# A hybrid encoder step whose 64-token sample is taken ahead of the prompt's chunks

## The reference

```
h = RMSNorm_pre(x)
proj = h @ w_in            # 7704 columns: q, k, v of two attentions, gate paths, pooling, 3 x 1024 merge gates
A: GLA linear attention, 4 heads, chunks of 64 in the reference, state (64 x 128) per head
B: causal pooling mixer
C: gated DeltaNet, 4 heads, state (128 x 128) per head:
   u = triangular_solve(1 + M, beta v - ...);  o = q_dec S + a_qk u;  S = g_last S + k_dec^T u
m = sum_b sigmoid(g_b) * (branch_b @ wo_b);   x = x + RMSNorm_post(m @ w_out)
```

## Time and profile before

| | us |
|---|---|
| median of 3 runs | 2552.24 |
| time of the profiled execution | 2555.57 |
| its span, first to last instruction | 2553.8 |
| PE matmul busy | 2476.2 (97%) |
| PE weight load busy | 2384.8 (93%) |
| DVE / ACT / POOL busy | 1041.3 / 674.8 / 820.7 |
| mean granted PE clock | 0.981 |
| bytes moved | 265.88 MB, mean 104 GB/s |

### The profile page before, as it was taken

How to read it: one execution, slowest core, us unless ns; L and a number is a source line. 1 busy time by engine, 2 the same in 40 slices (tenths; PEclk the granted TensorE clock), 3 DMA queues, 4 the chain that set the end, 5 groups by cost and what they waited for, 6 DMA issues and landing times. The chain is left out here.

```text
span 2553.8 us, 40027 instructions
## 1 busy us (share of the span) xinstructions
PE 2476.2 (97%) x15943; PEld 2384.8 (93%) x15943; DVE 1041.3 (41%) x1603; ACT 674.8 (26%) x1349; POOL 820.7 (32%) x711
## 2 busy tenths in 40 slices
PE   7999999999999999999999999999999979999998
PEld 7989999999999999998999999999999869999886
DVE  6620111134465662005554554545555443325332
ACT  6211111111255521113222332222332232223221
POOL 1211221121211212215545555445555213334222
PEclk9999999999999999999999999999999879999999
DMA  4213521111112122411432326432224345553543
GB/s 163 73 68 110 212 76 50 42 52 42 42 51 76 51 82 88 139 59 46 117 110 79 84 82 208 133 100 81 82 81 110 104 165 212 178 183 129 159 144 99
DMA packets 200200, 265.88 MB, mean 104 GB/s; under 512 B 16177, under 2 KB 175297, under 8 KB 194433
## 3 DMA queue, kind: packets, MB, share of 16 engines
q1 hardware_dynamic: 200064, 263.86, 32.1%
HBM read 164.54 MB, written 99.29 MB: 103 GB/s over the span
## 5 line engine op out<-in xcount | busy, mean ns | idle before, releaser
L178 POOL TENSOR_TENSOR w_hi<-w_raw,zero 128x1024 fp32r<-128x1024 f32 x77 | 148.3, 1926 | 1188.9 <-PE dense L348 824.8
L346 PE MATMUL dense<-h_hi_first,w_hi 128*128 128x352 f32 x1032 | 341.2, 331 | 0.7 <-POOL w_lo L180 0.7
L347 PE MATMUL dense<-h_lo_first,w_hi 128*128 128x352 f32 x1032 | 334.1, 324 | 0.0
L347 PE MATMUL dense<-h_lo_second,w_hi 128*128 128x352 f32 x1032 | 334.0, 324 | 0.0
L348 PE MATMUL dense<-h_hi_first,w_lo 128*128 128x352 f32 x1032 | 334.0, 324 | 0.0
L348 PE MATMUL dense<-h_hi_second,w_lo 128*128 128x352 f32 x1032 | 333.2, 323 | 0.0
L346 PE MATMUL dense<-h_hi_second,w_hi 128*128 128x352 f32 x1032 | 332.3, 322 | 0.0
L1360 PE MATMUL gate_bank<-h_hi_first,w_hi 128*128 128x352 f32 x768 | 275.7, 359 | 12.4 <-issue 5.1
L1360 PE MATMUL gate_bank<-h_hi_first,w_lo 128*128 128x352 f32 x768 | 250.4, 326 | 0.0
L1360 PE MATMUL gate_bank<-h_lo_first,w_hi 128*128 128x352 f32 x768 | 250.3, 326 | 0.0
L2205 PE MATMUL y<-o_hi,wo_hi 128*128 128x352 f32 x576 | 187.7, 326 | 14.2 <-DVE wo_lo L2249 12.8
(11 more groups left out here) (234 smaller groups left out, 4765.1 us busy)
## 6 DMA issues: line engine op xcount, KB each, us to landing
w_raw<-in_w_in SPq DMA_DIRECT2D x77, 512.0 KB, 5.8
rows_then_inputs<-scratch_feat SPq DMA_DIRECT2D x16, 1856.0 KB, 9.2
scratch_feat<-row_y SPq DMA_DIRECT2D x28, 1056.0 KB, 4.9
gate<-scratch_gates SPq DMA_DIRECT2D x12, 2112.0 KB, 8.5
scratch_gates<-gate_row SPq DMA_DIRECT2D x96, 176.0 KB, 2.3
o_raw<-scratch_branch_out SPq DMA_DIRECT2D x6, 2112.0 KB, 13.0
scratch_merged<-merged SPq DMA_DIRECT2D x48, 176.0 KB, 1.9
rows_then_inputs<-in_x_prompt SPq DMA_DIRECT2D x16, 512.0 KB, 3.6
```

Of the source, the lines that this page charges most:

```text
L178: nc.gpsimd.tensor_tensor(self.hi[:, p], raw, zeros, ALU.add).then_inc(self.high_ready, 1)
L346: nc.tensor.matmul(out, w_hi[:, p, k], h_hi[:, k, cols], start=(k == 0), stop=False)
L347: nc.tensor.matmul(out, w_hi[:, p, k], h_lo[:, k, cols], start=False, stop=False)
```

## The change

The sample's chunk is taken first (number 0), the prompt's chunks follow as 1 to 16. Each of the 17 chunks now issues six gate tiles. The two half blocks that the sample's chunk makes (the first half of the tokens of gate blocks 6 and 7) are no longer made in the projection, which ends with their second half only, written out as six tiles; their weights stay in place between the stages. The half change comes at chunk 8. The sample's states are loaded at the start of the stage; behind the sample SP stores them, and DVE sets the state buffers to zero in chunk 1 (`zero_states`). The closing stage's first loads are issued after the last gate store of chunk 16, and behind them the prompt's states and the last outputs are stored. Where a chunk has one level fewer, the counts of the semaphores are made up at the start (`missing`).

```diff
 # project_phase, PE
-                with pe.Fori(0, 1 + EARLY_GATES // 2) as i:
+                with pe.Fori(0, EARLY_GATES // 2) as i:
                     conv_project(i * 2 + 10, 1)
                     conv_project(i * 2 + 11, 0)
+                for n in range(TILES):
+                    u, t = n // 3, n % 3
+                    if t == 0:
+                        pe.wait_ge(w_split, F_LATE - 1 + u)
+                    pe.wait_ge(act_free, (A_GATE + EARLY_GATES - 2) * TILES + n - 1)
+                    ...  # 24 matmuls on hi[1], lo[1]
 # project_phase, POOL
-                pool.wait_ge(dense_ready, (F_LATE - 1) * TILES)
-                weights.split(nc, pool, F_LATE // 2, F_LATE, 1)
 # project_phase, SP
-                for c in range(2):
-                    first.load(sp, d, c, c)
+                first.load(sp, d, CHUNKS, 0, NS_)
+                first.load(sp, d, 0, 1)
 # chunk_phase, SP
+                sp.wait_ge(state_zero, 1)
+                sp.dma_start(state[:, :, :], d["state_gdn"]...).then_inc(state_landed, 16)
+                for h in range(HEADS):
+                    sp.dma_start(gla_state[half_of(h), h], d["state_gla"][h]).then_inc(state_landed, 16)
+                gate_traffic(0, 0, None)
+                store_states(0, "new_gdn_sample", "new_gla_sample")
+                store(0, CHUNKS, NS_)
+                load(1, 0)
                 ...
-                gate_traffic(CHUNKS - 1, 1, None)
-                store(CHUNKS - 1)
-                ...  # prompt states stored, waited for, sample states loaded
+                gate_traffic(CHUNKS - 1, 1, 1)
+                store(CHUNKS - 1, CHUNKS - 2)
+                gate_traffic(CHUNKS, 1, None)
                 ...
                 late.load_in_chunk_phase(sp, d)
-                store(CHUNKS, NS_)
-                ...  # sample states stored
+                store_states(CHUNKS, "new_gdn_prompt", "new_gla_prompt")
+                store(CHUNKS, CHUNKS - 1)
 # chunk_phase, all engines
+            SAMPLE, FIRST, SECOND = (0, 0, 0, NS_), (1, 0, 1, P), (2, 1, 0, P)
+            LAST = (CHUNKS, CHUNKS // 2, 0, P)
+                chunk(SAMPLE, FIRST)
+                chunk(FIRST, SECOND)
+                with eng.Fori(1, CHUNKS // 2) as i:
                     chunk((i * 2, i, 0, P), (i * 2 + 1, i, 1, P))
                     chunk((i * 2 + 1, i, 1, P), (i * 2 + 2, i + 1, 0, P))
+                chunk(LAST, None)
 # chunk, PE
-                        for g in range(steps[0], 0 if sample else steps[0] + count):
+                        for g in range(steps[0], steps[0] + count):
                     ...
                     if L < LEVELS:
+                        gate_products(3)
                         key_turns()
                         state_read()
 # chunk, DVE
+                def zero_states():
+                    dve.wait_ge(state_stored, 5 * 16)
+                    nc.vector.memset(state[:, :, :], 0.0)
+                    nc.vector.memset(gla_state[:, :, :], 0.0).then_inc(state_zero, 1)
+                    if isinstance(c, int) and c == 1:
+                        zero_states()
 # chunk_phase, POOL, opening
-                split_gate_w(0, 1)
-                queries(*FIRST_CHUNK)
+                queries(*SAMPLE)
```

More of the change, by code:

```diff
@@ L464, in _ @@
                 conv_project(9, 0, square_sums(7))
-                with pe.Fori(0, 1 + EARLY_GATES // 2) as i:
+                with pe.Fori(0, EARLY_GATES // 2) as i:
                     conv_project(i * 2 + 10, 1)
                     conv_project(i * 2 + 11, 0)
+                for n in range(TILES):
[3 more added lines that the diff above has]
+                    pe.wait_ge(act_free, (A_GATE + EARLY_GATES - 2) * TILES + n - 1)
+                    out = dense[:, n % 2, 0:TW]
+                    for k in range(KD):
+                        cols = slice(t * TW, (t + 1) * TW)
+                        nc.tensor.matmul(out, w_hi[:, 1 - u, k], hi[1][:, k, cols], start=(k == 0), stop=False)
+                        nc.tensor.matmul(out, w_hi[:, 1 - u, k], lo[1][:, k, cols], start=False, stop=False)
+                        mm = nc.tensor.matmul(out, w_lo[:, 1 - u, k], hi[1][:, k, cols], start=False, stop=(k == KD - 1))
+                    mm.then_inc(dense_ready, 1)
             @block.scalar
@@ L688, in _ @@
                         gate_block(i, i * 2 + (F_GATE + 1 - p), p)
+                for n in range(TILES):
+                    p, t = 1 - n // 3, 3 + n % 3
+                    if t == 3:
+                        act.wait_ge(gate_stored[p], (EARLY_GATES // 2 - 1) * 16)
+                    act.wait_ge(dense_ready, (F_LATE - 2) * TILES + n + 1)
+                    nc.scalar.copy(Y[:, p, t * TW:(t + 1) * TW], dense[:, n % 2, 0:TW]).then_inc(act_free, 1)
             @block.vector
@@ L1202, in levels_of, with missing @@
             return n.bit_length() - 1
+        def missing(n):
+            return LEVELS - levels_of(n)
         with nc.Block() as block:
@@ L1341, in chunk @@
                     L = levels_of(n)
-                    sample = then is None
+                    sample = n == NS_
                     steps = [0]
@@ L1454, in chunk @@
                             gate_products(2)
-                        if l == 3 and not sample:
+                        if l == 3 and then is not None:
                             now(pe, "diag_taken", c)
@@ L1491, in chunk @@
                     now(pe, "U_taken", c)
-                    if not sample:
+                    if then is not None:
                         now(pe, "gb_taken", then[0])
@@ L1544, in gates_out @@
                 def gates_out(c, t):
-                    if isinstance(c, int) and c == CHUNKS:
-                        return
                     act.wait_ge(gate_ready, c * TILES + (t + 1))
@@ L1629, in split_gate_w @@
                 def split_gate_w(c, r):
-                    weights.split(nc, pool, c + (F_LATE + r) // 2, c * 2 + (F_LATE + r), slot(r))
+                    weights.split(nc, pool, c + (F_LATE + r) // 2 - 1, c * 2 + (F_LATE - 2 + r), slot(r))
                 def queries(c, i, p, n):
@@ L1651, in chunk @@
                     I = inputs[:, p]
-                    gates = then is not None and then[3] == P
+                    gates = then is not None
                     now(pool, "dec_ready", c)
@@ L1742, in keys, with chunk @@
                     last.then_inc(S["KF_ready"], 1)
-                def chunk(this, then, opening=False):
+                def zero_states():
+                    dve.wait_ge(state_stored, 5 * 16)
+                    nc.vector.memset(state[:, :, :], 0.0)
+                    nc.vector.memset(gla_state[:, :, :], 0.0).then_inc(state_zero, 1)
+                def chunk(this, then):
                     c, i, p, n = this
@@ L1862, in _ @@
                 preload(dve, DVE_)
+                dve.sem_inc(z_taken, missing(NS_))
+                dve.sem_inc(xt_updated, missing(NS_))
                 dve.sem_inc(pairs_masked, 1)
-                decay_columns(*FIRST_CHUNK)
-                gate_sums(*FIRST_CHUNK)
-                gate_diffs(*FIRST_CHUNK, range(LEVELS))
+                decay_columns(*SAMPLE)
+                gate_sums(*SAMPLE)
+                gate_diffs(*SAMPLE, range(LEVELS))
                 dve.wait_ge(masks_landed, 16)
-                chunk(FIRST_CHUNK, (1, 0, 1, P), opening=True)
-                chunk((1, 0, 1, P), (2, 1, 0, P))
-                per_chunk(dve, chunk, 1)
+                per_chunk(dve, chunk)
 class LateWeights:
```

144 lines of the change are left out of this document (65 added, 79 removed).

## The result

The changed kernel takes 2581.48 us (median of 4 runs, 2579.36 to 2584.68); the kernel before, on the same chip, 2552.81 (2550.89 to 2554.39). The ratio is 1.0116, interval 1.0103 to 1.0128: slower by 29 us where 6 us less were forecast, and outside the range. The spans are 2582.7 and 2553.8, so the traces hold the whole difference.

What follows compares the result with a forecast made beforehand. PE, busy to nine tenths, was taken as the bound, SP's queue as second limit. Terms -23.1 - 0.3 + 46.0 - 9.5 + 0.5 + 1.9 - 21.7 = -6.2 took the median from 2552.24 to 2546.0 us; range 2537 to 2553.

Steps and rivals of the forecast that it cites:

- part 5: Half change and chunk loop: six loop starts cost PE 1.9 us each, none now hidden in the half change; +1.9 us.
- C: Sample's and first full chunk: POOL late in both, DVE waits for att and PE for Z; +8.2, 2560 us; chance 0.10.
- Part 1: Projection: two half gate blocks, six tiles, leave it, -23.1 us, and the hand-over wait shrinks by 0.3.
- Part 2: Sample's chunk, now first and with gate products, KK to KK: adds 46.0 us, bounds 44.2 to 53.7.
- 1.75 of waits: Sample's chunk: 0.75 us for DVE's late k_tok and 1.0 for less cover in short levels.
- 8.5 saved by 64 tokens: Sample's chunk: being 64 tokens wide takes 8.5 us off a full chunk's 52.67, leaving 44.2.
- KK's ratio of 0.65: Sample's chunk: KK matmuls 64 wide last 0.68 against 1.05 us; this ratio guided the estimate of a level's own part.
- Part 3: First full chunk: becomes an ordinary one, 52.67 instead of 62.20 us; -9.5, bounds -9.5 to 0.
- Part 4: SP's queue behind the sample: late inputs idle PE by 0.5 us, 0 to 6.7; DVE never waits for state stores.
- Part 6: End: gap from last gate product to first closing matmul falls from 55.4 to 33.7 us, stores landing behind loads; -21.7.
- Rival A: End: stores do not queue behind loads, the gap is 24.6 us; total -15.3, 2537 us; chance 0.13.

Runs made afterwards that it cites:

- 32 fillers: The changed kernel with 32 idle semaphore increments on PE at the end of the projection, ahead of the chunk loop: 2540.62 us, ratio 0.9956.
- good places: Loop head moved into seven blocks by idle semaphore increments in PE's opening: kernel before with 112, 2546.44 us; changed kernel with 16, 2539.62 us.
- 144 fillers: The changed kernel with 144 idle semaphore increments on PE at the end of the projection, ahead of the chunk loop: 2577.31 us.

## Why the prediction was wrong

**The failed step is part 5**, "Each start of a further loop round costs PE ... 1.9. There are six. ... again six starts". I took the price from one period of the kernel before and carried it over as a constant. It is a price of the place of the loop's head: 0 in seven blocks, 11.8 us for the whole loop in the place of before (754.9 against 743.2), 45.6 in that of after (788.9 against 743.3). The change writes six tiles' and two chunks' instructions ahead of the loop and so moved the head by 96 places in its block, out of a poor place into the worst of those measured. This term, +34.0 in place of +1.9, is 32.1 of the 35.1 us by which the span's difference was missed (-6.2 forecast, +28.9 measured). None of the rivals had it; C named a slower outcome by POOL, and in the sample's and the first full chunk neither PE nor DVE waits for POOL.

**Part 1 was right**: 23.1 + 0.3 forecast, 24.8 measured; the hand-over gap is 4.65 against the 4.63 of the earlier trace rows. Where the other 1.4 came from I have not resolved; the first KK varies by up to 2 us among the runs of the changed kernel that have no more than 32 fillers.

**Part 2, +46.0, was mis-sized by 4.0.** Two errors partly cancel. The 1.75 of waits did not come: from 1128.68 to 1178.73 PE is busy 49.88 of 50.05 us. So the work itself is 49.9, not 44.2, and my 8.5 saved by 64 tokens are only 2.8. The changes between 64 and 128 rows are 2.0 of the 5.7 by the estimate above; the rest is not tested, only read from the timeline, in gate portions that follow 64-wide matmuls (1.63 instead of 1.53) and in groups whose 64 columns save less than KK's ratio of 0.65 said.

**Part 3 was right**, 52.91 forecast 53.2 with part 4. **Part 4**: PE has no wait for late inputs, nor DVE one for the state stores ahead of the zeroing.

**Half change**: part 5's +1.9 was the jump that it no longer hides. In good places, where a jump costs nothing, its two periods are 6.2 over two plain ones (57.14 + 54.35), and 5.8 for before (57.27 + 53.82): +0.4, under the bounds of 1.3 to 3.6.

**Part 6 was right**, 33.85 for 33.7, and step by step: with E = 2070.7, the loads start at E + 2.4 (2.6 forecast), the last gate load lands at E + 25.1 (25.0) and the last store at E + 27.7 (27.6). Rival A, stores that do not queue behind loads, would have shown about 25 and is refuted for this queue twice: by that gap, and by 22.2 once the stores go first. The Trainium skill, "DMA: Bandwidth & Descriptors", section "Queues, rings and completion order", says that completion is not first in, first out for one issuing engine; the trace of the kernel after does not show it, since each of the seven stores landed behind all the loads ahead of it.

At equal places the sum without part 5's jumps and with the sample as measured would be -4.1; the traces say -4.9 and the medians -6.8. What I could have read beforehand: the count of PE's instructions in a loop round, the packets of the instruction queue (112, though the loop is run seven times), and that the diff puts instructions ahead of a loop with 5.1 us of idle "issue".

## What to carry to other kernels

A gap before the first instructions of a loop round that nothing releases was here a fetch of instructions (the profile can also put it down to another engine, as it did to ACT); count the round's instructions and the place of its head, and move the head with a few idle instructions before judging any change that adds code ahead of it. Compare two kernels only with their loops in equally good places, else a diff is credited with its layout. Ahead of a stage's last wait, issue what that wait needs before anything large that it doesn't.

## What the runs showed of the hardware

- PE held a loop of 1670 instructions over seven blocks of 256 without fetching any of it (no packet from 1326 to 1978 us), and not over eight (51 packets). The Trainium skill, "Advanced Engine Details and Errata", section "ISA Cache", gives TensorE 128 KB in lines of 256 instructions: eight lines, of which the runs show seven usable for a loop. The same section's two lines are not what TensorE shows here.
- With eight blocks a jump cost 2.0 to 3.4 us of its period with 144 fillers, and 6.3 to 6.8 with none. By the steps found above, which put the boundary 1 to 16 instructions behind after's head, the head lies 128 to 143 behind a boundary with 144 fillers. At one jump of the kernel after, gaps of 1.54 and 2.89 us were followed by 6.8 us at 1.2 GHz, which added 2.1 to this period and 1.1 to the next.
- A semaphore increment on PE's queue took 0.15 us when many follow each other; at the hand-over 32 of them added nothing to the gap, 96 added 8.9 us, 136 added 15.2.
- Changing between fp32 operands of 64 and 128 rows cost PE 0.14 us a time (six changes fewer: 49.22 instead of 50.06 us).
- 256 KB stored on SP's queue landed 13.1 us after their issue behind 7872 KB of loads, and 2.3 us after it ahead of them.
